# All high-weight passes of a weight chunk ahead of its low-weight passes, with a new order of work in the scan and at the start of the feed-forward, in a two-block model on one core

## The reference, cut to what matters

```python
def first_block(...):                       # h: 272 x 1024
    h = h + rms_norm(hybrid_mixer(rms_norm(h)))      # conv branch + stick-breaking attention
    u, g = split(rms_norm(h) @ w_up_gate)            # 2 x 2816 columns
    h = h + rms_norm((gelu(causal_dwconv(u)) * g) @ w_down)
def second_block(...):                      # x: 256 x 1024
    # even layer: one product with w_in, cut into z_a, xbc, dt, q, k, v, gate, g
    #   SSD scan over x, b, c (16 heads), gated by silu(z_a), normed
    #   gated linear attention over q, k, v (8 heads), normed, gated by silu(g)
    x = x + concat(ssd, gla) @ w_out
    # odd layer: q, k, v, z from w_in; attention of 16 heads; gated by silu(z)
    x = x + (attention * silu(z)) @ w_out
    return rms_norm_2(x, final_norm)
```

## Time and profile before

| | |
|---|---|
| median of 3 runs | 846.91 us (846.84 to 847.1) |
| the profiled execution's own time | 846.78 us |
| its span, first to last instruction | 844.9 us |
| TensorE busy with matmuls | 98% of the span |
| TensorE busy with weight loads | 95% |
| VectorE, ScalarE, GpSimd busy | 74%, 60%, 14% |
| mean granted TensorE clock | 0.998 |

### The profile page before, as it was taken

One profiled execution on the slowest core, in us unless ns is written; L12 is line 12 of the kernel. 1 busy time (PEld: TensorE's weight loads), 2 busy tenths in 40 slices (PEclk: granted clock), 3 DMA queues, 4 the chain that ended last, 5 costly groups with the idle time before them and its releaser, 6 DMA issues.

```text
span 844.9 us, 16864 instructions
## 1 busy us (share of the span) xinstructions
PE 830.4 (98%) x6770; PEld 799.7 (95%) x6770; DVE 622.5 (74%) x1055; ACT 504.9 (60%) x876; POOL 120.2 (14%) x119
## 2 busy tenths in 40 slices
PE   8999999999999999999999999999999999999997
PEld 7999999999999999999999999998898999888896
DVE  6647888886666688677664488999797696568765
ACT  6346657555454576555554468797868555356655
POOL 1000000000000305433441100042414010000002
PEclk9999999999999999999999999999999999999999
DMA  8744435445555536655666535545444376654431
GB/s 307 254 153 141 154 104 173 128 138 175 187 181 193 173 101 193 196 188 179 195 194 187 192 101 166 176 153 184 149 152 153 114 229 183 191 169 136 125 101 50
DMA packets 39853, 139.81 MB, mean 165 GB/s; under 512 B 4432, under 2 KB 5088, under 8 KB 39648
## 3 DMA queue, kind: packets, MB, share of 16 engines
q1 hardware_dynamic: 37728, 135.22, 50.1%
q10 hardware_dynamic: 2048, 3.51, 1.3%
HBM read 137.65 MB, written 1.06 MB: 164 GB/s over the span
## 4 chain that ended last, share of the span: by engine, by line
PE 82%; DVE 9%; ACT 5%; issue 1%; DMA 1%; POOL 1%; SPq 0%; DVEq 0%; ACTq 0%; POOLq 0%
PE ps L1806 66%; PE ps L1834 4%; PE ps L1809 4%; DVE weights_lo L1077 3%; ACT weights_hi L549 1%; PE ps L1949 1%; PE ps L1934 1%; DMA raw_weights<-weights_in 1%; PE ps L1963 1%; PE ps L2217 1%; PE ps L2235 1%; DVE arena L1388 1%; PE ps L2225 1%; POOL arena L479 0%; ACT arena L888 0%
## 5 line engine op out<-in xcount | busy, mean ns | idle before, releaser
L1077 DVE TENSOR_TENSOR weights_lo<-raw_weights,weights_hi 128x1024 fp32r<-128x1024 f32 x251 | 311.8, 1247 | 87.1 <-ACT weights_hi L549 86.8
L1806 PE MATMUL ps<-x_hi,weights_hi 128*128 128x256 f32 (+3 forms) x1272 | 367.8, 289 | 1.2 <-DVE weights_lo L1077 0.5
L1806 PE MATMUL ps<-x_lo,weights_hi 128*128 128x256 f32 (+3 forms) x1272 | 358.1, 282 | 0.0
L1806 PE MATMUL ps<-x_hi,weights_lo 128*128 128x256 f32 (+3 forms) x1272 | 357.9, 281 | 0.0
L549 ACT ACTIVATE weights_hi<-raw_weights 128x1024 fp32r<-128x1024 f32 x251 | 263.2, 1053 | 147.6 <-PE ps L1806 61.0
L1806 PEld LDWEIGHTS ps<-x_hi,weights_hi 128*128 128x128 f32 x1272 | 239.2, 188 | 8.7 <-issue 6.0
L1806 PEld LDWEIGHTS ps<-x_lo,weights_hi 128*128 128x128 f32 x1272 | 239.6, 188 | 0.7 <-issue 0.5
L1806 PEld LDWEIGHTS ps<-x_hi,weights_lo 128*128 128x128 f32 x1272 | 239.5, 188 | 0.0
L1806 PE MATMUL ps<-y_hi,weights_hi 128*128 128x256 f32 (+1 forms) x488 | 137.7, 282 | 0.0
L1806 PE MATMUL ps<-y_lo,weights_hi 128*128 128x256 f32 (+1 forms) x488 | 137.4, 282 | 0.0
L1806 PE MATMUL ps<-y_hi,weights_lo 128*128 128x256 f32 (+1 forms) x488 | 137.1, 281 | 0.0
(11 more groups left out here) (268 smaller groups left out, 1069.9 us busy)
## 6 DMA issues: line engine op xcount, KB each, us to landing
raw_weights<-weights_in SPq DMA_DIRECT2D x251, 512.0 KB, 3.8
arena<-decay_rows ACTq DMA_DIRECT2D x8, 256.0 KB, 3.9
masks<-masks_in SPq DMA_DIRECT2D x1, 1186.0 KB, 7.1
raw_weights<-weights_in SPq DMA_DIRECT2D x4, 256.0 KB, 6.0
hidden<-xT_in SPq DMA_DIRECT2D x2, 272.0 KB, 6.7
hidden<-xT_in ACTq DMA_DIRECT2D x1, 276.0 KB, 4.0
hidden<-xT_in ACTq DMA_DIRECT2D x1, 272.0 KB, 5.9
gate_w<-gate_w_in ACTq DMA_DIRECT2D x1, 256.0 KB, 3.7
```

The costliest lines, as they stand in the source:

```text
L1077: d.sig(TT(wlo[:, s * CW:(s + 1) * CW], raw[:, (c % RAW) * CW:(c % RAW + 1) * CW], whi[:, s * CW:(s + 1) * CW].bitcast(F32), ALU.subtract) ...
L1806: ins = mm(bank(BANK_OF[no])[:, 0:b - a], wt, x_[:, kt, a:b], start=s0, stop=s1)
```

## The change

Three edits, each in the order of work only. No operation is added or taken out, apart from waits.

1. In `project`, each chunk is now gone through twice: first whi*xhi and whi*xlo of all its blocks, behind a wait for `hi_ready`; then wlo*xhi of all of them, behind a wait for `lo_ready`. `ready(kt)` is called in the first of these. So `ready(7)` of a tile of one chunk is met after 14 matmuls instead of 21.
2. In the scan, round 1: ScalarE's `take_keys(1)` moves from behind `feed(("ez", 3))` to behind `feed(("eg", 2))`; VectorE's `gla_states(1)` and `conv_in(("ex", 5))` move from the end of the round to right behind `feed(("eg", 3))`. Rounds 2 and 3: ScalarE's `feed(("ev", p))` moves ahead of `gla_exps(p)`; VectorE's `ssd_args(u)` moves ahead of `feed(("eq", p))`.
3. At the start of the feed-forward VectorE's `ffn_conv(1)` moves ahead of `feed(("fu", 1))`.

```diff
@@ ScalarE, the scan
                     gla_squares(p - 1)
+                    feed(("ev", p))
                     gla_exps(p)
-                    feed(("ev", p))
                     take_values(p)
...
                 feed(("eg", u))
+                if p == 1:
+                    take_keys(1)
                 half_tanh(("eg", u), gs[:, u % 4, :])
...
                 feed(("ez", u + 1))
-                if p == 1:
-                    take_keys(1)
@@ VectorE, the feed-forward
             ffn_conv(0)
+            ffn_conv(1)
             feed(("fu", 1))
-            ffn_conv(1)
@@ VectorE, the scan
                 else:
+                    ssd_args(u)
                     feed(("eq", p))
                     z_full(("ex", u + 1), xs[:, u + 1, :], name="xsilu")
-                    ssd_args(u)
...
                 feed(("eg", u + 1))
+                if p == 1:
+                    gla_states(1)
+                    conv_in(("ex", 5))
                 z_full(("ez", u + 1), zs[:, 1, :])
...
                 if p == 1:
                     decay_sums(1)
-                if p < 3:
-                    conv_in(("ex", u + 3))
-                gla_states(p)
+                else:
+                    if p < 3:
+                        conv_in(("ex", u + 3))
+                    gla_states(p)
@@ TensorE, project
+                while j0 < nb:
+                    c = (f + j0) // BPC
+                    j1 = min(nb, (c + 1) * BPC - f)
+                    for w_, parts, signal in ((whi, (hi, lo), "hi_ready"), (wlo, (hi,), "lo_ready")):
+                        pe.wait_ge(S(signal), c + 1)
+                        for j in range(j0, j1, step):
+                            kt, at = j // step, (c % RING) * CW + ((f + j) % BPC) * P
+                            if w_ is whi and ready is not None:
+                                ready(kt)
...
+                    if j1 < nb:
                         ins.then_inc(S("chunk_read"), 1)
+                    j0 = j1
```

More of the change, by code:

```diff
@@ L1791, in project @@
                 step = 1 if toks is None else nb // KT
[L1792 to L1802, removed]
-                            wt = w_[:, at:at + step * P]
[L1804 to L1813, removed]
@@ new lines, in project @@
+                outs = [None] if toks is None else toks
+                j0 = 0
+                while j0 < nb:
[7 more added lines that the diff above has]
+                                ready(kt)
+                            first, last = j == 0 and w_ is whi, j + step >= nb and w_ is wlo
+                            wt = w_[:, at:at + step * P]
+                            for o, tok in enumerate(outs):
+                                for m, part in enumerate(parts):
+                                    s0 = first and m == 0
+                                    if tok is None:
+                                        ins = mm(bank(BANK_OF[no])[:, 0:b - a], wt, part[:, kt, a:b],
+                                                 start=s0, stop=last)
+                                    else:
+                                        t0, t1 = tok
+                                        ins = mm(bank(BANK_OF[no + o])[0:t1 - t0, 0:step * P], part[:, kt, t0:t1], wt,
+                                                 start=s0, stop=last)
+                                if last:
+                                    ins.then_inc(S("out_ready"), 1)
+                    if j1 < nb:
```

## The result

The changed kernel takes 850.3 us (850.03 to 850.53, 6 runs) against 846.88 (846.84 to 847.18, 6 runs): ratio 1.0039, 95% interval 1.0029 to 1.0049. It is slower by 3.4 us; 849.6 was predicted, in a range of 843.6 to 851.0.

A forecast was written before the change was run, and what follows sets the result against it. TensorE was taken as the bound, busy 830.4 of 844.9 us. Passes +0.7 and round 3 +2.0 gave +2.7 on 846.78, 849.5, and with 0.13 up to the median 849.6 us; range 843.6 to 851.0.

The forecast's parts named there:

- The largest term: Round 3: ScalarE stands ahead of `ev`'s second split, delaying heads 14 and 15: +2.0 us, between +1.5 and +2.3.
- Round 1 is worth nothing: Both TensorE waits (1.5 and 1.3 us) go, but the 3.1 us lead shrinks to about 0.1 by `gla_out(2)`: gain 0.
- The rival "faster": Scan: `gla_states(2)` ends at 627.3 or before, TensorE keeps a lead and most stalls go: -3.3, 843.6 us; chance 0.20.
- In round 2 the same edit costs nothing: Early `feed(ev)` in round 2: TensorE leads by up to 3.1 us and has left `ev2` when the second split comes.
- `mk0` and `mq1`: Calls met earlier: block 7 of `mk0` waits 0.6 plus 0.15 for the signal, +0.75; `m_scores(0)` in `mq1`, +0.13.
- `fg1` and `ex0`: Sums `total(2)` and `total(3)` met earlier: stalls of 0.65 and 0.5 to 0.6 us, net -0.46 and +0.3.
- do not move with TensorE: After `fg1`: the waits at 323.45 and 326.86 stay put, so the delay of about 0.6 us is given back.
- I take 0: Passes in `project`: one wait more for each of about 250 chunks costs 0; upper bound 5 us in all.
- only TensorE's idle time can change: Whole kernel: no matmul is taken out, so only TensorE's 14.5 us of idle time can change.
- Edit 3 at 0: Feed-forward's start: `ffn_conv(1)` delays a low half some 0.9 us, hidden by 16 matmuls: 0; without cover up to 0.9.
- 0.3, 0.46 and 0.9: Range's upper end: 2.3 for 2.0 in round 3, 0 for the -0.46 of `fg1`, 0.9 for edit 3.

The follow-up runs named there:

- four-tile run: Changed kernel with the tiles `fg1`, `ex0`, `mk0` and `mq1` made block by block by the old `project`: 848.15 us, ratio 1.0014.
- both repairs: Changed kernel with `fg1`, `ex0`, `mk0`, `mq1` block by block as before and `feed(ev)` back behind `gla_exps` in round 3 alone: 846.05 us, ratio 0.9989.
- the first two columns of the table: TensorE's lag against the kernel before: the changed kernel (850.3 us), and the kernel before with only the new passes in `project` (848.15 us).
- the halves' sum: Two runs against the kernel before: only the new passes in `project`, 848.15 us (+1.2); only the scan's new order, 849.06 us (+2.1).

## Why the prediction was right

**The largest term, +2.0 in round 3, was right in place, mechanism and size.** Alone it measured +2.1, undone alone -2.2. The stand of ScalarE was 1.75 us and not 2.0. The rest of the 2.60 by which the masks' factors moved is the 0.47 by which ScalarE came into this stretch later (L893 at 633.30 instead of 632.83), 0.15 ahead of the first split (from 633.88 to 634.03), and 0.2 for the two splits, which stood apart (1.06 each) instead of back to back (2.00 for both). TensorE at the heads moved by 2.46, and had been 0.28 late before. The exponentials began only when the split that waited was nearly done (637.80, the split from 636.84 for 1.06). That they did not pass it agrees with the rule on strict queues in the Trainium skill (TensorE: Matmul & The Clock Gate, section on the architectural detail of the array).

**Round 1 is worth nothing: right.** Both waits went, and at `gla_out(2)` TensorE was 0.28 late where 0.1 early was forecast; the scan's order without round 3's edit measured no difference. The rival "faster" failed at the point it named: `gla_states(2)` ended at 629.23, not before 627.3. What I had not seen is how the lead is given back. It matters that it goes in pieces: in one piece of 3.81 us it took the clock down and 1.0 us with it. "In round 2 the same edit costs nothing" held, and said too little: against `feed` late there, it wins 1.0.

**`mk0` and `mq1`.** At `mk0` TensorE's lag grows from 2.6 behind the scan to 3.37 (the first sums behind `mk0`, L1865, began at 704.90, after at 708.27): 0.75, as forecast, though not in the forecast's parts: TensorE was held for 0.6 in all, of which the signal took 0.06 (706.93 to 706.99) and not 0.15, and the first matmul behind the stand took 0.22 to the next one instead of 0.12. At `mq1` the lag grows by 0.15 (3.28 to 3.43), 0.13 forecast. Another 0.1 comes bit by bit between 760 and 810 us, with no wait of its own.

**`fg1` and `ex0`: right in sum, on a wrong footing.** The forecast was -0.46 and +0.3. TensorE came to the feed-forward 0.72 late and left `ex0` about 0.5 late, -0.2 in all: -0.67 up to `fu4`, +0.13 on the way, +0.30 at `ex0`. But I booked the stalls as absorbed by waits that "do not move with TensorE". They would have gone anyway, and the four-tile run shows that without the stalls the new heads win there what they can. The stalls' true price was about 1.3 us: 2.15 less 0.75 and 0.15 is 1.25, and behind `ex0` the four-tile kernel is 1.32 ahead of the changed one (0.70 of it from `fg1`).

**The step that was missing: the drift.** "I take 0" for the passes held for the waits (with one wait the kernel was no faster) but not for the matmuls: 0.8 us between 43 and 265 us that no term had. The premise "only TensorE's idle time can change" failed there: TensorE was busy throughout and did less. Nothing took it back. The feed-forward's start gives 1.1 us to a TensorE that comes late (1.20 to 0.05) and to one that comes early (-0.27 to -1.37), and taken out of the version with both repairs, the drift showed at the end: 1.53 us under the kernel before instead of 0.94, and 0.97 between the two traces. That the sum was off by 0.7 alone is in part luck: the stretch up to `fu4` gave 0.2 more than forecast, and the medians have the passes at 1.16 where the two traces have 1.46.

**Edit 3 at 0: right**, by the run of it alone and by the first two columns of the table.

The forecast of 849.6 is 0.7 short of 850.3: by 0.5 in the passes (1.16 measured for 0.7), by 0.1 in the scan, and by the 0.2 that the halves' sum lacks (3.2 of 3.4). The range's upper end was added up too low: 849.6 with 0.3, 0.46 and 0.9 is 851.3, not 851.0; the result lies inside either.

## What to carry to other kernels

Before a step that waits is moved ahead of one that doesn't, ask on both sides: what it waits for at its new place, and what is queued behind it there. The same line can pay in one round of a loop and cost in the next, because the lead of the engine that it waits for differs; edit the rounds apart. Where an order of passes is changed, list the calls that are hung on a block's number: each is met earlier or later by the passes in between, and keep the old order for those whose input is only just in time.

## What was not expected of the hardware

- An idle stretch of TensorE of 3.81 us was followed, 1.5 us after work began again, by 3.2 us at a granted clock of 0.50 (1.2 GHz). Waits of up to 1.5 us in the changed kernel were not; its mean clock is 0.998 as before.
- Two orders of the same matmuls, with all of them ready, ran 0.5% apart in the first block (760 and 756 in 90 us) and within 0.1% in the feed-forward (0.11 us in 105). It is neither the second wait (756 with one) nor the order of the two high-weight passes (755). Nor is it the number of columns alone: matmuls of 258 columns start 119.3 ns apart before and 120.0 after between 43 and 265 us, but 119.8 in both between 330 and 435. What it is stays open.
